# Hybrid mLSTM and S5 layer with SwiGLU FFN: sums of weight blocks by adding transfers, and GpSimd's other FFN arithmetic on VectorE

## The reference

```python
hf = rmsnorm(x, g_ffn)
x = x + (jax.nn.silu(hf @ w_ff1) * (hf @ w_ff3)) @ w_ff2     # 1024 -> 2816 -> 1024
...
y = rmsnorm(x, norm_final_g)
```

## Time and profile before

| | |
|---|---|
| median of 3 runs | 1010.9 us (1008.11 to 1015.56) |
| profiled execution, its time | 1013.47 us |
| its span, first to last instruction | 1011.7 us |
| mean granted TensorE clock | 0.962 of full |
| TensorE busy | 925.9 us (92%) |
| VectorE busy | 750.1 us (74%) |
| ScalarE busy | 509.9 us (50%) |
| GpSimd busy | 499.2 us (49%) |
| moved by DMA | 112.49 MB, mean 111 GB/s |

### The profile page before, as it was taken

One profiled execution on the slowest core, in us unless ns is written; L12 is line 12 of the kernel. 1 busy time (PEld: TensorE's weight loads), 2 busy tenths in 40 slices (PEclk: granted clock), 3 DMA queues, 4 the chain that ended last, 5 costly groups with the idle time before them and its releaser, 6 DMA issues. The chain is left out here.

```text
span 1011.7 us, 20752 instructions
## 1 busy us (share of the span) xinstructions
PE 925.9 (92%) x8550; PEld 890.7 (88%) x8550; DVE 750.1 (74%) x1028; ACT 509.9 (50%) x862; POOL 499.2 (49%) x512
## 2 busy tenths in 40 slices
PE   8999999999999999999999788887998887998795
PEld 4899998998998999999999688886998887998795
DVE  7879964955954967434347689998789998789893
ACT  5578377468469575233334354453444443344441
POOL 6888958246240210000016856664456664556556
PEclk9999999999999999999999998998999897999878
DMA  7423264343353345333243022222222222222112
GB/s 296 149 82 108 69 230 153 147 169 116 126 199 106 116 155 210 125 96 109 89 148 104 1 84 84 84 85 84 84 85 84 84 85 84 84 84 73 63 33 84
DMA packets 36804, 112.49 MB, mean 111 GB/s; under 512 B 3524, under 2 KB 7668, under 8 KB 34792
## 3 DMA queue, kind: packets, MB, share of 16 engines
q1 hardware_dynamic: 32032, 79.91, 23.4%
q0 software_dynamic: 2736, 24.13, 6.4%
...
HBM read 97.78 MB, written 13.39 MB: 110 GB/s over the span
## 5 line engine op out<-in xcount | busy, mean ns | idle before, releaser
L554 ACT ACTIVATE w_high<-raw 128x1024 fp32r<-128x1024 f32 (+1 forms) x137 | 142.8, 1047 | 157.0 <-PE G L1921 91.2
L1333 DVE TENSOR_TENSOR w_low<-raw,w_high 128x1024 fp32r<-128x1024 f32 x78 | 98.1, 1264 | 80.5 <-ACT w_high L554 79.9
L1775 DVE TENSOR_TENSOR w_low<-raw,w_high 128x1024 fp32r<-128x1024 f32 (+1 forms) x59 | 135.1, 2289 | 27.2 <-ACT w_high L554 27.2
L2243 PE MATMUL G<-ffn_in_high,w_high 128*128 128x260 f32 x308 | 93.2, 303 | 45.0 <-ACT up_a L554 36.8
L1921 PE MATMUL G<-h_high,w_high 128*128 128x256 f32 (+1 forms) x640 | 131.1, 286 | 0.0
L1921 PE MATMUL G<-h_low,w_high 128*128 128x256 f32 (+1 forms) x640 | 129.0, 283 | 0.0
L1921 PE MATMUL G<-h_high,w_low 128*128 128x256 f32 (+1 forms) x640 | 128.9, 283 | 0.0
L2243 PEld LDWEIGHTS G<-ffn_in_high,w_high 128*128 128x128 f32 x308 | 62.7, 204 | 47.6 <-issue 43.7
L1921 PEld LDWEIGHTS G<-h_high,w_high 128*128 128x128 f32 x640 | 99.3, 188 | 2.0 <-issue 1.6
L1921 PEld LDWEIGHTS G<-h_low,w_high 128*128 128x128 f32 x640 | 99.2, 188 | 0.0
L1921 PEld LDWEIGHTS G<-h_high,w_low 128*128 128x128 f32 x640 | 99.2, 188 | 0.0
...
## 6 DMA issues: line engine op xcount, KB each, us to landing
raw<-wst SPq DMA_DIRECT2D x116, 512.0 KB, 3.8
c_samples<-c POOLq DMA_DIRECT2D x4, 2048.0 KB, 8.8
out_cs<-c_samples POOLq DMA_DIRECT2D x4, 2048.0 KB, 7.9
w_sums<-wst SPq DMA_DIRECT2D x15, 512.0 KB, 4.9
...
w<-wst SPq DMA_DIRECT2D x8, 512.0 KB, 4.4
x_tokens<-xt SPq DMA_DIRECT2D x4, 520.0 KB, 5.2
...
```

Of the source, the lines that this page charges most:

```text
L554: return act.activation(out, in_, ACT.Copy, **kw)
L1333: tt(WL[n.slot()][:], raw[n.slot()][:], WH[n.slot()][:].bitcast(F32), ALU.subtract).then_inc(w_lo, 1)
L1775: tt(halves_of(WL[w_at(q)], r), halves_of(round_source(r, i), r), halves_of(WH[w_at(q)], r).bitcast(F32), ALU.subtract).then_inc(w_lo, 1)
L2243: last = mm((G, Q)[su][:, bank, 0:HALF], w[s][:, c], h[:, RHS[i], k, :], start=start and i < 3 and k == ks[0] and t == 0, stop=stop and k ...
```

## The change

The sign of three operands is turned so that only additions remain: unit 3 becomes a21 + a22 + a11, unit 4 a11 + a21, unit 5 a21 + a22 + a11 + a12. Each addition is a transfer issued from GpSimd that reads a block of the weights from DRAM and adds it to what stands in the tile (accum_op). In FB three of them follow each other in a round: on a21 first a22, then a11 after unit 0 is split, then a12 after unit 3 is split. In BB a21 is added to a11 after unit 1 is split. GpSimd issues them in the order sum_first(r), sum_12(r), sum_22(r + 1), sum_11(r + 1). a22 alone has now one tile, raw[0], and is loaded one unit after unit 6 of the round before was split.

GpSimd does no more arithmetic in the FFN but the identity tile. VectorE gets, before the first round, the combinations of inputs and the additions of squares; in each up round the two subtractions for up_a and up_b (between the low splits of the next units 0 and 1), the multiply of up_b by frq (right behind that of up_a), and two scalar_tensor_tensor where tensor_tensor stood; in the last round the additions of squares; after it all 16 scalings, in place of 10. TensorE sums part of the squares inside the last product, and spreads each inverse root once and not twice. Stores of y alternate between SyncE and ScalarE.

```diff
-        EB = [sb("w_22", [P, U], at=at_w3 + 12 * U), raw[0]]
-        BB, DB = raw[1], raw[2]
+        EB, BB, DB = raw
...
-            return (FB[r % 2], BB, DB, FB[r % 2], BB, FB[r % 2], EB[r % 2])[i]
+            return (FB[r % 2], BB, DB, FB[r % 2], BB, FB[r % 2], EB)[i]
...
             def load_a22(r):
-                sp.dma_start(halves_of(EB[r % 2], r), block_of(r, 1, 1)).then_inc(a22_in[r % 2], 16)
+                sp.dma_start(halves_of(EB, r), block_of(r, 1, 1)).then_inc(a22_in, 16)
 
             n = N_FF - 4
             sp.wait_ge(w_lo, n - RING + 1)
             load(At(n))
             sp.wait_ge(unit_done, N_OUT)
             load_a21(0)
-            load_a22(0)
             for n in range(N_FF - 3, N_FF):
                 sp.wait_ge(w_lo, n - RING + 1)
                 load(At(n))
             sp.wait_ge(w_lo, N_FF - 2)
             load_a11(0)
+            load_a21(1)
             sp.wait_ge(w_lo, N_FF - 1)
             load_a12(0)
+            sp.wait_ge(w_lo, N_FF)
+            load_a22(0)
             for r in range(1, NR):
                 before = N_FF + UNITS_R * (r - 1)
-                if r == 1:
-                    sp.wait_ge(w_lo, N_FF)
-                else:
-                    sp.wait_ge(w_lo, before - UNITS_R + 6)
-                load_a21(r)
-                if r >= 2:
-                    sp.wait_ge(w_lo, before - UNITS_R + 7)
-                load_a22(r)
+                sp.wait_ge(w_lo, before + 3)
+                load_a12(r)
                 sp.wait_ge(w_lo, before + 5)
                 load_a11(r)
-                sp.wait_ge(sums, 4 * (r - 1) + 4)
-                load_a12(r)
-            for half, m, count in [(1, m, m + 1) for m in range(5)] + [(0, m, 6 + m) for m in range(5)]:
-                sp.wait_ge(y_dve, count)
+                sp.wait_ge(w_lo, before + 6)
+                if r + 1 < NR:
+                    load_a21(r + 1)
+                sp.wait_ge(w_lo, before + 7)
+                load_a22(r)
...
-                if i == 0 or 3 <= i < 6:
-                    act.wait_ge(sums, 4 * r + (1, 0, 0, 2, 3, 4)[i])
+                if i in (0, 3, 5):
+                    act.wait_ge(s_in[r % 2], 48 * (r // 2) + 16 * (1 + (0, 3, 5).index(i)))
                 elif i == 1:
                     act.wait_ge(a11_in, 16 * r + 16)
                 elif i == 2:
                     act.wait_ge(a12_in, 16 * r + 16)
-                else:
-                    act.wait_ge(a22_in[r % 2], 16 * (r // 2) + 16)
+                elif i == 4:
+                    act.wait_ge(s3_in, 16 * r + 16)
+                else:
+                    act.wait_ge(a22_in, 16 * r + 16)
...
-                take(4, x, 7, took_x4)
+                take(4, x, 7, took_x4, -1.0)
...
-            def sum_up(r, step):
-
-                f, b, d, e = (halves_of(x, r) for x in (FB[r % 2], BB, DB, EB[r % 2]))
-                unit = N_FF + UNITS_R * r
-                if step == 0:
-                    pool.wait_ge(a21_in[r % 2], 16 * (r // 2) + 16)
...
-            for m in range(KC):
-                part = DT[:, 4 * (m % 2):4 * (m % 2) + 4, :]
-                pool.wait_ge(xg_ready, KC + m + 1)
-                if m >= 2:
-                    pool.wait_ge(hl_ready, KC + (m - 1 if m < 6 else 2 * m - 6))
-                if m < 4:
-                    tt(part[:, 0, :], XS[:, m, H1], XS[:, m, H0], ALU.subtract).then_inc(t_ready, 1)
-                else:
-                    own.do(tt(part[:, 1, :], XS[:, m, H1], XS[:, m - 4, H1], ALU.subtract))
-                    own.do(tt(part[:, 2, :], part[:, 1, :], XS[:, m - 4, H0], ALU.add))
-                    tt(part[:, 3, :], XS[:, m, H0], part[:, 2, :], ALU.subtract).then_inc(t_ready, 1)
-                if m >= 1:
-                    pool.wait_ge(sq_ready, KC + m + 1)
-                    if m >= 2:
-                        pool.wait_ge(sq_added, 1 + m)
-                    tt(facc[:], fsq[0][:] if m == 1 else facc[:], fsq[m % 2][:], ALU.add).then_inc(sq_added, 2 if m == 1 else 1)
-                if m == 3:
-                    sum_up(0, 0)
-                if m == 6:
-                    sum_up(0, 1)
...
-            for r, (kind, _, _) in enumerate(ROUNDS):
-                u = up_index(r)
-                sum_up(r, 2)
-                sum_up(r, 3)
-                if r < NR - 1:
-                    sum_up(r + 1, 0)
-                    sum_up(r + 1, 1)
-                if kind == "up":
-                    for su, (p5, u3) in enumerate(((DT[:, 2, :], DT[:, 7, :]), (CB[:, 2, :], CB[:, 3, :]))):
-                        pool.wait_ge(took_z0, 2 * r + su + 1)
-                        pool.wait_ge(took_x4, 2 * r + su + 1)
-                        tt(p5, p5, u3, ALU.add).then_inc(c22_ready, 1)
-                    if u == 0:
-                        pool.wait_ge(inverse_ready, 3)
-                    pool.wait_ge(c22_ready, 2 * u + 2)
-                    pool.wait_ge(took_y2, 2 * r + 2)
-                    pool.wait_ge(took_z5, 2 * r + 2)
-                    tt(CB[:, 0:3, :], CB[:, 0:3, :], frq[:, 0:3, :], ALU.mult).then_inc(b_early, 1)
...
-            for i in range(1, 4):
-                pool.wait_ge(sq_ready, 2 * KC + i + 1)
-                if i > 1:
-                    pool.wait_ge(sq_added, 1 + KC + i - 1)
-                tt(facc[:], sqf[0][:] if i == 1 else facc[:], sqf[i][:], ALU.add).then_inc(sq_added, 1)
-            for i in range(4):
-                part = facc[:, (H0, H1)[i // 2]]
-                pool.wait_ge(sq_ready, 2 * KC + 4 + i + 1)
-                pool.wait_ge(sq_added, 1 + KC + 3 + i)
-                tt(part, part, sqh[i][:], ALU.add).then_inc(sq_added, 1)
-            for count, half in enumerate((1, 0)):
-                pool.wait_ge(inverse_copied, count + 1)
-                for m in range(5, KC):
-                    own.do(tt(X1[:, m, (H0, H1)[half]], X1[:, m, (H0, H1)[half]], inv_sb[:, half, :], ALU.mult))
-                    pool.tensor_scalar(X1[:, m, (H0, H1)[half]], X1[:, m, (H0, H1)[half]], g_fin[:, m:m + 1], None, ALU.mult).then_inc(y_pool, 1)
+            def add_block(tile, r, row, col, s):
+
+                pool.dma_start(halves_of(tile, r), block_of(r, row, col), accum_op=ALU.add).then_inc(s, 16)
+
+            def sum_22(r):
+                pool.wait_ge(a21_in[r % 2], 16 * (r // 2) + 16)
+                add_block(FB[r % 2], r, 1, 1, s_in[r % 2])
+
+            def sum_11(r):
+                pool.wait_ge(s_in[r % 2], 48 * (r // 2) + 16)
+                pool.wait_ge(w_lo, N_FF + UNITS_R * r + 1)
+                add_block(FB[r % 2], r, 0, 0, s_in[r % 2])
+
+            def sum_first(r):
+                pool.wait_ge(a11_in, 16 * r + 16)
+                pool.wait_ge(w_lo, N_FF + UNITS_R * r + 2)
+                add_block(BB, r, 1, 0, s3_in)
+
+            def sum_12(r):
+                pool.wait_ge(s_in[r % 2], 48 * (r // 2) + 32)
+                pool.wait_ge(w_lo, N_FF + UNITS_R * r + 4)
+                add_block(FB[r % 2], r, 0, 1, s_in[r % 2])
+
+            sum_22(0)
+            sum_11(0)
+            for r in range(NR):
+                sum_first(r)
+                sum_12(r)
+                if r + 1 < NR:
+                    sum_22(r + 1)
+                    sum_11(r + 1)
...
+            def combine_input(m):
+
+                part = DT[:, 4 * (m % 2):4 * (m % 2) + 4, :]
+                if m < 4:
+                    tt(part[:, 0, :], XS[:, m, H0], XS[:, m, H1], ALU.subtract).then_inc(t_ready, 1)
+                else:
+                    own.do(tt(part[:, 1, :], XS[:, m, H1], XS[:, m - 4, H1], ALU.subtract))
+                    own.do(stt(part[:, 2, :], part[:, 1, :], -1.0, XS[:, m - 4, H0], ALU.mult, ALU.subtract))
+                    stt(part[:, 3, :], part[:, 2, :], -1.0, XS[:, m, H0], ALU.mult, ALU.subtract).then_inc(t_ready, 1)
+
+            def add_square(m):
+                dve.wait_ge(sq_ready, KC + m + 1)
+                if m >= 2:
+                    dve.wait_ge(sq_added, 1 + m)
+                tt(facc[:], fsq[0][:] if m == 1 else facc[:], fsq[m % 2][:], ALU.add).then_inc(sq_added, 2 if m == 1 else 1)
...
+                dve.wait_ge(xg_ready, KC + m + 1)
+                combine_input(m)
                 if n + RING < N_FF:
                     low(At(n + RING))
                 for q in ((0, 1), (2,), (3,))[m - 5] if m >= 5 else ():
                     split_low(q)
+                if m >= 1:
+                    add_square(m)
...
-                    dve.tensor_copy(frq[:, 2:4, :], frq[:, 0:2, :]).then_inc(inverse_ready, 1)
+                    own.add(dve.tensor_copy(frq[:, 2, :], frq[:, 0, :]))
+                    ts(frq[:, 3, :], frq[:, 1, :], -1.0, None, ALU.mult).then_inc(inverse_ready, 1)
+                    own.settle()
                     dve.wait_ge(inverse_ready, 3)
                 next_low(r, 3)
+                for su, (p5, u3) in enumerate(((DT[:, 2, :], DT[:, 7, :]), (CB[:, 2, :], CB[:, 3, :]))):
+                    dve.wait_ge(took_z0, 2 * r + su + 1)
```

(29 more changed lines are left out.)

110 lines of the change are left out of this document (53 added, 57 removed).

## The result

The changed kernel takes 979.98 us (median of 4 runs, 978.07 to 981.25) against 1009.81 us of the kernel before, run beside it (4 runs, 1008.11 to 1015.56): a ratio of 0.9693, 95% interval 0.9651 to 0.9736. The forecast was 969 with a range of 930 to 1018; the gain is 29.8 us of the 41 expected. The profiled execution took 978.07 us; its span of 976.3 is 35.4 us less than the span before.

A forecast was written before the change was run, and what follows sets the result against it. In the FFN TensorE waits on a chain through VectorE, slowed by GpSimd's sums, and ScalarE, losing about 93 us. 38 us won there and 4 in the tail: 1013.5 less 42 is 971.5, forecast 969 by the median, range 930 to 1018.

The forecast's parts named there:

- VectorE's speed: In the FFN, without GpSimd's sums, VectorE runs at fast rows: 1.21 us for 1024 columns, 0.95 for 780.
- STT at 1.4 times a tensor_tensor: Two VectorE operations per up round become scalar_tensor_tensor: 0.574 us at 256 columns against 0.41, 0.3 for both.
- The chain: Up round, last product through VectorE, hidden_low and ScalarE's copies to the fourth product: its 4.7 us wait becomes 0.15 to 0.25.
- T: The end of a round's last product on TensorE, from which the chain's times are counted.
- The adding transfer: GpSimd's transfers into the weight sums: issue to landing (A) taken as 6.0 us, between 3.0 and 8.8.
- the first rival: Adding transfers hide, landing in up to 5.2 us, say 4.4: 72 + 4 us won, 935 us; chance 0.25.
- Rival 2: Additions become the bound: at 8.8 us landing 1021 us, slower than before from about 8.3; chance 0.15.
- Rival 3: VectorE not freed, slowed by landing additions or GpSimd's descriptor writing: 23 us more, 1034; chance 0.05.
- under 1 us each: GpSimd's transfer issues, four per round, take under 1 us each and hide on an otherwise empty engine.
- The sum: FFN loss of TensorE's time falls from 93 to 55 us, 38 won; the tail wins 4 more.
- restarts: After a long wait TensorE's first 12 matmuls run at half clock, 2.94 us for 1.45: 1.5 us per restart.
- they have 6 us and more of slack: The next round's a22 and a11 additions, queued on GpSimd behind the third, have 6 us and more to spare.

The follow-up runs named there:

- two_halves: The changed kernel with each round's third addition (a12) cut into two half-width transfers, the second issued only when the first has landed; 1055.76 us.
- a22_first: The changed kernel with GpSimd issuing the next round's a22 addition ahead of this round's third addition; 988.14 us.
- no_third: The changed kernel with the third addition of each round (a12 onto w_sums, for unit 5) left out, its wait on GpSimd kept; 927.59 us.
- sbuf_add: The changed kernel with a12 loaded plainly and the running sum added onto it from SBUF, not waiting for unit 3's low split; 930.86 us.

## Why the prediction was right, point by point

**VectorE's speed** was the reason of the gain, as forecast, and every duration came out at the fast row: w_low of 1024 columns 1.22 us on average, 780 columns 0.96, hidden_low of 520 columns 694 ns. By the runs it is GpSimd's reading that stops VectorE. The Trainium skill says this ("SBUF — State Buffer", Who interferes with whom): an operation of VectorE with two SBUF inputs contends with one of GpSimd that reads SBUF, not with one that only writes it. The Trainium skill adds (the same page, SBUF: two separate sides) that the one that starts first has the pair of ports that the two share for the whole instruction, and the other blocks. The runs agree on the contention and on the blocking: beside 4.97 us of reading, 4.4 us longer; beside fills, 1190 ns as ever; and the takes, with one input in PSUM, at 0.41 us beside GpSimd's sum. That whoever starts first goes on unhindered isn't visible in these rows, in which both of the lengthened operations are recorded as started ahead of GpSimd's (whose recorded spans are rough).

**STT at 1.4 times a tensor_tensor** was wrong and small. With an immediate scalar, 260 columns take 0.43 us against 0.42 (758.57 and 758.92 above). The 574 ns of rows 9 are the mean of 64 operations of another form, with a scalar column, of which 47 take 472 to 481 ns; the 17 others, 540 to 1258 ns, all lie beside two-input operations of GpSimd, and of the 47 none lies beside one of more than 32 columns. So the row that priced the form held the very contention that the prediction is about. The Trainium skill's rule of half throughput, which was weighed there, is not borne out by these rows either.

**The chain.** With T = 755.2, last x6 at T+1.3 (forecast T+0.75), hidden_low out at T+7.15 (T+6.9), the second take at T+9.1 (T+8.85). The fourth product waits 0.2 to 0.5 us in six of the eight rounds (0.15 to 0.25), and 1.6 and 1.5 in two.

**The adding transfer** was taken at 6.0 us between 3.0 and 8.8; it measured 5.8 (6.3 onto raw). It is worth seeing how: the line through the rows of GpSimd's plain reads, counted at twice the bytes, gave 5.8; for 256 KB the same line gives 4.3, and 4.3 was measured in two_halves. The rule of the Trainium skill ("DMA: Bandwidth & Descriptors", Anatomy of one DMA) gave 4.4 and with it the first rival's 935, which fell. In the engines' time an adding transfer costs 2.1 times a plain one per byte: the software queue's time rose from 65 to 279 us for 34.6 MB more, 6.2 us per MB, where SP's queue spent 238 us on 79.6 MB, 3.0 per MB.

**Rival 2** had the direction right, as two_halves shows, but not its size: a straight line from 5.7 us and 980 to 9.2 and 1056 would put the tie with the kernel before near 7.1 us, not at 8.3. That is an estimate from two runs that differ in more than the landing time. **Rival 3** is out: w_low stays fast beside 0.76 of DMA load and all the issues of GpSimd. Of these, "under 1 us each" was low: an adding issue takes 1.2 us. It cost nothing on the empty engine.

**The sum.** The spacing of TensorE's matmuls gives what it loses: the length of the rounds less 0.12 us for each matmul, which is their distance where nothing is waited for. By kinds of rounds, in the two profiles (the column "won" is from the lengths of the stretches):

| | lost before | lost after | forecast after | won, forecast | won |
|---|---|---|---|---|---|
| 11 up rounds | 65.0 | 36.4 | 34.5 | 30.5 | 28.6 |
| 6 down rounds | 37.0 | 35.5 | 20.8 | 7.2 | 1.5 |
| after the last product | | | | 4 | 3.2 |
| ahead of the first product | | | | 0 | 2.0 |

(The losses in the last down round hold 2 to 3 us of small products for the squares, before and after. The forecast didn't split its 93 us; less the measured 65.0 they leave 28.0 for the down rounds, and less 20.8 that is 7.2.) The last column adds up to 35.3 of the 35.4 us between the spans. The 2.0 ahead of the first product are mostly chance: that product starts between 561.7 and 563.3 us in the four profiles of kernels built on the one before, and between 559.6 and 563.1 in the eight of the changed kernel's kind. Between the medians it is 29.8, because the profiled execution before stood 3.7 above its median and the one after 1.9 below its own.

In the forecast's own terms, waits and restarts, the kernel before lost 67 and 27 us against its 93, and the changed kernel 48 and 15, 63 in all, where 55 had been forecast. The up rounds came out near the forecast, partly by luck: the waits at the fifth product are 2.1 to 2.5 us against 2.0, and two of eight are followed by a restart where one had been counted for each. The down rounds won almost nothing, and that is most of the miss; the wait rows say how. TensorE's waits for hidden_low fell from 14.2 to 4.4 us, as forecast, but those for the residual adds rose from 7.5 to 17.0. Group by group, the two first waits of a down round (hidden values, second take) are 0.4 and 1.4, 2.0 and 1.4, 2.0 and 0 where 1.55 was forecast for both; the one behind the third addition is 2.7, 2.7 and 1.9 where 2.7 was forecast; the one in the second down round is 2.2, 1.8 and 3.0 where 1.0, 1.0 and 2.3 was forecast. That is some 4 us of waits too few. Most of the rest is the restarts: 8.9 us at the lower level in the down rounds, where 3 had been counted. Before the change it was 10.8 there, so only 2 us of them were won.

One step that failed is "they have 6 us and more of slack", of the next round's additions. The a22 addition is issued right behind the third one (the x2 in GpSimd's row), and of two in flight the second lands late, after 8.7 us in the median: issued at 785.5 in a later round, it landed after 10.7 us and was waited for by ScalarE up to 796.22, and at the end of that group hidden_low came at T+8.6.

```profile
796.22 1.06 ACT L550 ACTIVATE w_high<-w_sums 128x1024 fp32r<-128x1024 f32 x1 [3.19 <-DMA w_sums<-wst]
```
```profile
810.32 0.39 PE L2238 MATMUL G<-hidden_high,w_high 128*128 128x260 f32 x1 [2.02 <-DVE hidden_low L1833]
```

The two waits of 1.6 and 1.5 us at the fourth product stand in rounds whose a22 addition took 10.5 and 10.4 us, and both are gone in a22_first. How much of the miss in the down rounds is due to it is not shown. Without the third addition 2.7 of the 4.4 us behind hidden_low stay, and the 1.4 at the second take too, so those are older than this change's transfers; and in a22_first, which put the a22 addition ahead, these pairs got no shorter (52.7 and 53.1 us). What no_third and sbuf_add do show is that the pairs of down rounds in the first two groups are 7.0 to 8.7 us shorter, of 51 and 52, once the third addition is off the chain: the forecast had 3.7 for it (2.7 and 1.0 of waits), and restarts.
